# A fused two-block kernel: the attention part, the output projection, the last two norms and the second down product rewritten token-major

## The reference

```
h = rmsnorm(x, g_norm1) * (1 + sc1) + sh1
proj = h @ w_in                      # q 512, k 128, v 128, z 1024 columns
q, k = rope(rmsnorm(q, g_q)), rope(rmsnorm(k, g_k))      # per head of 64
attn = softmax(q k^T * 64 ** -0.5) v                     # 8 query heads, 2 key heads
u, v = split(gelu(z));  v = rmsnorm(v, g_tok_v)          # per head of 64
tok  = u * (w_s @ v + b_s)                               # in chunks of 128 tokens
mixed = concat(rmsnorm(attn, g_attn_out), rmsnorm(tok, g_tok_out))
x = x + gt1 * (mixed @ w_out)
h = rmsnorm(x, g_norm2) * (1 + sc2) + sh2
a, b = split(conv3(h @ w_up));  x = x + gt2 * ((silu(a) * b) @ w_down)   # 2816 wide
out = rmsnorm(x, g_final)
```

## Time and profile before

| | us |
|---|---|
| median of 3 runs | 857.83 |
| the profiled execution | 856.17 |
| its span, first to last instruction | 854.4 |
| PE busy in the span | 793.8 (93%) |
| DVE / ACT / POOL busy | 569.7 / 469.9 / 208.8 |
| mean granted clock of PE | 0.97 of full |

### The profile page before, as it was taken

The page is one execution under the profiler, slowest core; times in us unless marked ns, Lnnn a source line. Parts: engine busy times, 40 slices in busy tenths (PEclk is TensorE's granted clock), DMA queues, the critical chain, the costliest instruction groups (busy, mean ns, idle before and its releaser), DMA issues.

```text
span 854.4 us, 15196 instructions
## 1 busy us (share of the span) xinstructions
PE 793.8 (93%) x5717; PEld 735.8 (86%) x5717; DVE 569.7 (67%) x814; ACT 469.9 (55%) x757; POOL 208.8 (24%) x177
## 2 busy tenths in 40 slices
PE   3999999998999899999999988987797999999997
PEld 2899999987999689998989877865786999999997
DVE  7985777743776566675656656785536798866663
ACT  4975554466665465444454446656454555555553
POOL 4000000001024012253242314433253321233320
PEclk9999999999999979999999988999996999999998
DMA  6463332153445757787776812345151666555521
GB/s 240 135 186 126 124 123 101 50 174 99 129 163 178 270 198 272 245 271 265 276 274 242 315 54 99 99 173 173 49 172 50 221 230 213 185 187 185 185 98 50
DMA packets 45719, 146.97 MB, mean 172 GB/s; under 512 B 9292, under 2 KB 10060, under 8 KB 45664
## 3 DMA queue, kind: packets, MB, share of 16 engines
q1 hardware_dynamic: 44544, 144.88, 50.0%
q10 hardware_dynamic: 1120, 1.34, 0.5%
HBM read 144.07 MB, written 1.05 MB: 170 GB/s over the span
## 4 chain that ended last, share of the span: by engine, by line
PE 71%; issue 9%; DVE 9%; POOL 5%; ACT 4%; DMA 1%; POOLq 0%; SPq 0%; DVEq 0%; ACTq 0%
PE ps L736 23%; PE ps L492 19%; PE ps L749 7%; PE ps L690 7%; POOL gl L2151 2%; PE ps L961 2%; POOL relu L2148 2%; DVE ada_acc L1883 1%; PE ps L538 1%; PE ps L664 1%; PE ps L552 1%; PE ps L567 1%; DVE prob L1970 1%; PE ps L794 1%; DMA vtk<-in_x 1%
## 5 line engine op out<-in xcount | busy, mean ns | idle before, releaser
L1511 DVE TENSOR_TENSOR wl<-raw,wh 128x1024 fp32r<-128x1024 f32 x200 | 258.0, 1292 | 143.1 <-ACT wh L1023 141.8
L1023 ACT ACTIVATE wh<-raw 128x1024 fp32r<-128x1024 f32 x220 | 231.1, 1053 | 110.3 <-DMA raw<-in_w_stream 57.7
L736 PE MATMUL ps<-xh,wh 128*128 128x256 f32 x720 | 209.7, 291 | 12.6 <-POOL xl L2141 7.7
L736 PE MATMUL ps<-xl,wh 128*128 128x256 f32 x720 | 206.0, 286 | 0.0
L736 PE MATMUL ps<-xh,wl 128*128 128x256 f32 x720 | 206.0, 286 | 0.0
L736 PEld LDWEIGHTS ps<-xh,wh 128*128 128x128 f32 x720 | 139.8, 194 | 18.5 <-issue 11.6
L736 PEld LDWEIGHTS ps<-xl,wh 128*128 128x128 f32 x720 | 139.8, 194 | 1.3
L736 PEld LDWEIGHTS ps<-xh,wl 128*128 128x128 f32 x720 | 140.1, 195 | 0.0
L492 PE MATMUL ps<-xh,wh 128*128 128x256 f32 (+1 forms) x416 | 123.1, 296 | 2.2 <-DVE wl L1511 1.1
L492 PE MATMUL ps<-xh,wl 128*128 128x256 f32 (+1 forms) x416 | 119.0, 286 | 0.0
L492 PE MATMUL ps<-xl,wh 128*128 128x256 f32 (+1 forms) x416 | 118.9, 286 | 0.0
(11 more groups left out here) (389 smaller groups left out, 1472.9 us busy)
## 6 DMA issues: line engine op xcount, KB each, us to landing
raw<-in_w_stream SPq DMA_DIRECT2D x220, 512.0 KB, 3.7
ada_w<-in_w_ada SPq DMA_DIRECT2D x48, 512.0 KB, 4.5
vtk<-in_x SPq DMA_DIRECT2D x2, 512.0 KB, 4.8
out<-ob SPq DMA_DIRECT2D x4, 256.0 KB, 2.0
u<-uT SPq DMA_DIRECT2D x16, 34.0 KB, 2.4
eepp<-in_s_mats SPq DMA_DIRECT2D x1, 512.0 KB
bti<-btr SPq DMA_DIRECT2D x16, 32.0 KB, 2.5
ws<-in_w_s ACTq DMA_DIRECT2D x1, 512.0 KB, 3.8
```

The costliest lines, as they stand in the source:

```text
L736: mm = nc.tensor.matmul(ps[:, bank, 0:SEQ], w, x, start=(k == 0), stop=(k == 3 * KD - 1))
L1023: nc.scalar.activation(wh[:, b % RING], raw[:, b % RING], ACT.Identity).then_inc(hi_done, 1)
L1511: V.tensor_tensor(wl[:, b % RING], raw[:, b % RING], wh[:, b % RING].bitcast(F32), ALU.subtract).then_inc(lo_dve, 1)
```

## The change

Stages are named by their blocks: n counts from B_IN2, then from B_OUT2.

- Block order: gate values (n = 0 to 3) and gates (4 to 7) first, then v, k, q. The gelu is applied as each block leaves PSUM. The token mix runs behind n = 9.
- The remainders of the 20 blocks are made by DVE; POOL has nothing in this part.
- The query's deviation isn't multiplied into q. It is got by two matmuls of two columns per tile (`q_stat`), as 128x2 numbers per token, and enters as the scale of the exponential and of the maxima. The key norm stays.
- Heads go in pairs. `scores(i)` issues for both token halves the even head (partitions 0 to 63) and the odd head (64 to 127) in turn. The probabilities aren't divided; `weigh_v` gives tokens on the partitions (8 matmuls of 64 columns per pair), `attended` divides, and `turn_attended` turns the result back (2 transposes per pair). Pairs 0 to 3 stand in slots n = 12 and 13 of the first half and n = 0 to 4 of the output projection.
- The output projection is token-major (12 matmuls of 512 columns a block), first the gate branch (n = 0 to 3), then the attention branch (n = 4 to 7), each in two halves of the columns. The branch norm is a per-token scale, applied with the gate row gt1 as the product leaves PSUM (`out2`, `gated_part`, `add_part`). For it `turn_y` transposes the residual into `y_tm`, and `gate_row` spreads gt1 over the partitions.
- Norm r2 and the last norm are token-major, by squares with an accumulator on ACT (`row_squares`); r2 uses `turn_normed` and `split` as n1 does.
- The second down product uses `rows_in`, and gt2 is spread by two matmuls. g_final comes as a row by DMA.
- SP issues the modulation's weights in other slots of the loop (`ADA_SHARE[q - 2]`, `ada_rows`).

The diff, cut to its core:

```diff
+OUT2_BANKS = ((0, 1), (0, 1), (6, 7), (4, 5))
-POOL2 = (B_IN2 + AHEAD, B_F2)
@@ PE
+            def q_stat(i):
+                for t in range(NT):
+                    mm = nc.tensor.matmul(ps[:, 2, 256 + 2 * (NT * i + t):258 + 2 * (NT * i + t)], qs[:, (i + 1) % 3, t * P:(t + 1) * P],
+                                          heads2, start=True, stop=True)
+            def scores(i):
+                    pe.wait_ge(S["exp_done"], 2 * i)
+                for t in range(NT):
+                    for n in range(2):
+                        r = 64 * n
+                        mm = nc.tensor.matmul(ps[:, 6 + n, t * SEQ:(t + 1) * SEQ], qf[r:r + 64, i, t * P:(t + 1) * P], k,
+                                              start=True, stop=True)
             for b in range(B_IN2, B_OUT2):
+                if n in (1, 2):
+                    turn_y(n - 1)
+                if n == 4:
+                    turn_zv(0)
+                    turn_zv(1)
+                if n == 5:
+                    gate_row()
+                if n == 12:
+                    swap_k()
+                    tok_ms()
+                    q_stat(1)
+                    scores(0)
+                if n == 13:
+                    q_stat(2)
+                    scores(1)
+                    turn_probs(0)
+                    turn_probs(1)
             for b in range(B_OUT2, B_F2):
+                if n == 2:
+                    pe.wait_ge(S["part_done"], NT)
+                def one(t, kk):
+                    pe.wait_ge(S["branch_lo"], QT * branch + k + 1)
...
+                if n < 2:
+                    scores(n + 2)
+                if n < 3:
+                    turn_probs(2 * n + 2)
+                    turn_probs(2 * n + 3)
+                if n < 4:
+                    weigh_v(n)
+                if 1 <= n < 5:
+                    turn_attended(n - 1)
-                down(B_F2 + 3 * j + 1, j - 1, "ff2_lo", i * 4 + j, i * 12, first=(j == 1))
+                rows_down(B_F2 + 3 * j + 1, j - 1, "ff2_lo", i * 4 + j, F2_BANKS, i * 12, first=(j == 1))
@@ ACT
-                                         bias=smax[:, h, 1, t:t + 1], scale=HD ** -0.5,
+                                         bias=smax[:, h, 1, t:t + 1], scale=q_scale[:, h // 2, t, h % 2:h % 2 + 1],
+            def square_sum(src, to):
+                nc.scalar.activation(*src, ACT.Square, accum_out=to).then_inc(act_step, 1)
@@ DVE
+            def attended(i):
+                step(V.reciprocal(ssum[:, 2 * i:2 * i + 2, :], ssum[:, 2 * i:2 * i + 2, :]))
+                V.tensor_tensor(ao[:, i, :].rearrange("p (t h e) -> p t h e", t=NT, h=2),
...
+            def gated_part(t, bank, branch, dh):
+                V.scalar_tensor_tensor(pieces[t], ps[:, bank, :], branch_rstd[:, NT * branch + t:NT * branch + t + 1],
+                                       gate1[:, dh * 512:(dh + 1) * 512], ALU.mult, ALU.mult).then_inc(S["part_done"], 1)
+            def add_part(t, dh, counts):
+                dve.wait_ge(S["part_done"], parts[0])
+                ins = V.tensor_tensor(y_tm[:, t, dh * 512:(dh + 1) * 512], y_tm[:, t, dh * 512:(dh + 1) * 512], pieces[t], ALU.add)
             for b in range(B_OUT2, B_F2):
+                if n in (2, 3, 4, 5):
+                    att_lo(n - 2)
+                if n < 3:
+                    maxima(2 * n + 2)
+                    maxima(2 * n + 3)
+                if 1 <= n < 5:
+                    attended(n - 1)
+                if n == 2:
+                    out2(1, 0, 0)
+                if n == 4:
+                    out2(3, 0, 1)
+                lo(b + AHEAD)
+                if n == 6:
+                    out2(5, 1, 0)
@@ POOL
-            for b in range(POOL2[0], B_OUT2 + AHEAD):
-                lo(b)
```

More of the change, by code:

```diff
@@ L316, in two_blocks @@
[L316 to L323, removed]
+            "s_done", "max_done", "exp_done", "pt_done", "pt_copied", "o_done", "ao_done", "ao_turned",
@@ L714, in _ @@
                 rows_in(b, mh[:, k, :], ml[:, k, :], WO_BANKS, last=(b == B_F1 - 1))
-            turn_normed("n1")
-            def sum_squares(tag, bank, n=KD, per=1):
-                for m in range(n):
-                    pe.wait_ge(*norm(tag, "sq", m // per + 1))
-                    mm = nc.tensor.matmul(ps[:, bank, 0:SEQ], ones, sq[:, m, :], start=(m == 0), stop=(m == n - 1))
-                mm.then_inc(NORM["var"], 1)
+            turn_normed("n1", (ln("n1", "norm_act"), ln("n1", "norm_act", 2), ln("n1", "norm"), ln("n1", "norm_act", 3)))
             def block(b, bank, name, value, t=0, h=xh, l=xl, first=META, order=range(KD), ready=None):
@@ new lines, in _ @@
+                if n == 4:
[3 more added lines that the diff above has]
+                    gate_row()
+                if n == 8:
+                    pe.wait_ge(S["row_ev"], 2)
+                    modulation(1, (NMOD - 1) * KD, None, 0, 5)
+                if n == 9:
+                    turn_v2()
+                    for m in range(QT):
+                        mix_tokens(m)
+                if n == 10:
+                    k_stat()
+                if n == 11:
+                    q_stat(0)
@@ L969, in up2 @@
+            turn_normed("r2", (ln("r2", "norm_act"), ln("r2", "norm_act", 2), ln("r2", "norm"), ln("r2", "norm", 2)))
             def up2(j, i=0, ready=None):
@@ new lines, in _ @@
+            for t in range(NT):
+                row_squares(t, 0)
+            for t in range(NT):
+                row_squares(t, 1)
+                row_root(t)
+            for half in range(2):
+                act.wait_ge(*ln("r2", "rstd"))
+                nc.scalar.activation(xn[:, 0, half * 512:(half + 1) * 512], y_tm[:, 0, half * 512:(half + 1) * 512], ACT.Identity,
+                                     scale=row_rstd[:, 0:1]).then_inc(LN["norm_act"], 1)
+            split("r2", tg_m, lambda m: gain[:, 1, m:m + 1], lambda m: mod[:, M_SH2 + m:M_SH2 + m + 1])
@@ L2049, in outer_taps @@
+            row_reciprocal("r2", 0)
+            row_reciprocal("r2", 1)
+            dve.wait_ge(*ln("r2", "rstd", 2))
+            for half in range(2):
+                V.tensor_scalar(xn[:, 1, half * 512:(half + 1) * 512], y_tm[:, 1, half * 512:(half + 1) * 512], row_rstd[:, 1:2], None, ALU.mult)\
+                    .then_inc(LN["norm"], 1)
+            split("r2", tg_m, lambda m: gain[:, 1, m:m + 1], lambda m: mod[:, M_SH2 + m:M_SH2 + m + 1])
             def outer_taps(j, i, which):
```

811 lines of the change are left out of this document (407 added, 404 removed).

## The result

The changed kernel takes 835.77 us (median of 4 runs, 831.28 to 837.25) against 857.74 before (4 runs, 856.32 to 859.41): ratio 0.9734, 95% interval 0.9693 to 0.9776. Five more runs of it, beside eleven of the kernel before, gave 835.77 again, the kernel before 854.60: ratio 0.9781, 0.9754 to 0.9807. Forecast were 842.3 in a range of 836.5 to 851.0, so the time fell out of the range at its fast end, by 0.7 us.

The account below looks back on a forecast made before the run. PE mostly bounds the kernel; its waits in attention and projection, norm r2 and the end can move. -9.6-3.3-0.9-1.7 = -15.5 off the profiled 856.17 gives 840.7; the median is 1.7 above, so 842.3, range 836.5 to 851.

Parts of the forecast that it names:

- term 1: Attention and output projection: PE's own work -2.9 and its waits -6.7, together -9.6 us; bounds 0 to -15.
- Term 3: Down product of the second feed-forward: blocks of 2.80 for 2.84, 22 x 0.04 = -0.9 us; bounds 0 and -2.2.
- Term 4: The end, behind the last matmul: 11.3 us in place of 13.0, -1.7; bounds 0 and -3.
- small ones: Attention and projection: two PE waits, for the swapped key's copy and pair 2's exponentials, 0.7 us together.
- the long wait: Output block 2 waits 5.2 us for block 0's banks; 1.7 of clock lost behind it, as much as before.
- the right mirror: Token mix, outputs alternating between column halves, ran side by side; taken for the scores: 4.2 us in place of 8.4.
- Term 2: Norm r2 to the first down block: 13.1 us lost in place of 16.4, -3.3; bounds 0 and -6.1.
- rival 1: Attention scores: the pairs run one behind the other, 3.8 of the 4.2 us come back: 846.1; chance 0.27.
- rival 2: Attention: waits only move, the pair chain costs PE 15.5 us as before: 851.9; chance 0.13.
- rival 3: Output projection: the loop at output block 2 closes in each of slots 2 to 5, three more waits: 863.0; chance 0.05.

Follow-up runs that it names:

- the combination: The changed kernel with four edits of order (gated sums first, last remainder behind the last sum, exponential table loaded early): 825.77 us, ratio to before 0.9653.
- The run with GpSimd: The changed kernel with the remainders of the 19 weight blocks on GpSimd again, as before: 845.37 us, ratio to before 0.9875.

## Why the prediction was right and wrong

**The forecast's mechanism held; its sum was 2.4 too small. The step that failed is the size of PE's own work in term 1: -2.9 forecast, -4.5 measured.** Terms 3 and 4 were 0.6 and 0.8 short as well; the waits fell by 0.6 less than I had. One by one:

- Waits: 8.8 forecast, 9.0 measured, all at places that I had named. (Before they were 15.5 in the first trace and 14.1 in the second, so on average PE's idle time fell by 6.1, not 6.7.) By place they were less exact, so the good total is partly luck: block 2 4.6 for 5.2, block 5 1.6 for 2.0, the second pair 0.3 for 0.9, the copy of the swapped key none; but the fourth pair, which waits for the exponentials of pair 2, 2.4, where the two "small ones" together had 0.7. There I missed that the last query deviations make ACT load the root's table and then the exponentials' again, 1.28 each; the combination took 1.4 of it away.
- The clock behind the long wait: I had it cancel, and it did. The block behind the first wait of the output projection took 4.44 before (behind 2.8 us of waiting, clock 0.62) and 4.45 now (behind 4.6, clock 0.61).
- Score pairs: 4.2 saved forecast; four pairs of 1.07 (starts) against eight heads of 1.05: 4.1. The token mix was the right mirror, and the run with both heads on one half shows that the halves do it. The Trainium skill, TensorE: Matmul & The Clock Gate, Part 3, has it that matmuls on different row groups of the array run concurrently. The traces agree: 1.07 for a pair on two halves, in either order, 1.92 to 2.02 on one.
- Work, the step that failed: -2.9 forecast. PE's busy time fell by 4.5 (104.1 and 105.7 before, 99.7 and 101.0 after) though its clock was a little lower. `gate_row`: 2.1 by the scores' price; from its start to the next instruction's, 537.43 to 538.75, is 1.3. Products of 64 partitions and 256 columns gave no price for one of 128 partitions and 512 columns. The token mix went from 2.8 to 2.0 of busy time and the query statistics from 3.1 and 3.5 to 2.7; neither stood in my list at all. Against them an output block takes 2.88, not 2.80, in four of the eight (+0.3), and the sums that went (L939) had 3.9 of busy time, not 4.2.
- VectorE's load: I said that the division would lose its stall, gave that no price, and looked for harm only in the load. The run with GpSimd puts 10 us on it. It is inside the forecast because I built the waits from unstalled durations, so the sum had it without naming it. (The remainders that moved are 19, blocks 135 to 153, not 20.)
- Term 2: -3.3 forecast, -3.4 measured, partly by luck. The lag counted from VectorE's list was 1 too long (the second half's reciprocal started 5.0 behind PE's last end, at 627.44, not 6.15), and what stands behind it took 0.8 longer than in n1.
- Term 3: -0.9 forecast, -1.5 measured. The down blocks gave what I said. The up blocks followed in part: 20 rounds of 0.026 are 0.5, where the bound had 1.3. The spread of gt2 took 1.3, not 2.1, and the modulation that it replaces 1.7; but the stretch ends 0.3 later behind the start of the last down block (3.36 for 3.08).
- Term 4: -1.7 forecast, -2.5 measured. VectorE's sums ended 4.1 behind the last matmul for my 4.6, at 0.69 each for 0.75. The root of the second half ended 6.25 behind it for 6.95: the first root, with its table, ended at 4.2 for 4.5, and two squares and the second root took 2.0 for 2.45.

Rows of the end, VectorE and ACT:

```profile
826.65 0.69 DVE L2215 TENSOR_TENSOR res<-res,qg 128x512 f32<-128x512 f32 x1
...
829.50 0.16 DVE L2157 RECIPROCAL hb<-hb 128x1 f32<-128x1 f32 x1 [0.41 <-ACT hb L1413]
829.70 1.41 DVE L2221 SCALAR_TENSOR_TENSOR ob<-res,hb,wst 128x512 f32<-128x512 f32 x2
```

```profile
825.86 1.28 ACT L1413 ACT_TABLE_LOAD   x1
827.15 0.29 ACT L1413 ACTIVATE hb<-hb 128x1 f32<-128x1 f32 x1
```

**The rest of the miss is mostly the reference.** 842.3 less 835.8 is 6.5: 2.4 of it is the sum above, 0.8 the start. The remaining 3.3 are about what the kernel before varies by: 15.5 off 857.8 is 842.3, but the same kernel had medians of 854.6, 855.0 and 855.6 in three later sets of eleven runs. By the second ratio, 0.9781 x 857.8 = 839.0, which the range holds. So it is partly chance that the time fell below the range.

**The low end of the range was also added up wrongly.** It was to be term 1 without the clock loss (-1.7) and with half the waits (-4.4), and term 3 at its bound (-1.3). That is 842.3-7.4 = 834.9, not 836.5, and the measured 835.77 lies above it.

**The rivals.** Series pairs (rival 1): excluded, 1.07 a pair. Waits only move (rival 2): they fell from 15.5 to 9.0. The closing loop (rival 3): not here; block 2 alone waits for its banks, and block 5 only 1.6, for its low part. But a loop is what the kernel before shows when VectorE takes the remainders, by another chain. The longest wait came at output block 2, ended by the `qg` of L2043, with 4.6 for "near 5". One thing in it was wrong: I took the wait as given by the dependences. It was given by a list, and one line moved takes it away.

## What to carry over

When a wait is found, look at the engine that ends it for idle time ahead of the chain, and at what in its list could run there: here 8 us of idle stood in front of two instructions that were ready. A step that waits for another engine (a remainder for its high part) must not stand ahead of a chain that the other engine waits for. And whether a part of a change pays depends on the rest: the same 19 instructions cost 11 us in one order and save 10 in the other, so undo a part in the new kernel and add it alone to the old one.

## What the runs showed of the hardware

- VectorE beside a remainder of GpSimd (128 x 1024 from two operands in SBUF, most of them 2.34 to 2.41): an instruction on two numbers a partition that starts beside it ends when it ends, 1.63 to 2.23 in place of 0.16, three times of three. So in these three the cost was what was left of the remainder, not the size of the instruction. Row maxima read from PSUM (L2024) beside the same remainders kept their 0.68. In the other direction, a modulation row that began 0.04 behind a remainder took its usual 1.28, and the remainder 3.55.
- Float32 products of 64 partitions that lie on different halves run side by side: 1.07 for four of 256 columns, in either order of issue, and 1.9 to 2.0 when all are on one half.
- A wait of 4.6 us of PE was paid twice: the twelve matmuls behind it took 4.45 at a granted clock of 0.61 (0.50 for the first 3.5 us), and 2.9 where no wait stood ahead of them. Behind the wait of 6.7 they took 5.25, all at 0.50.
- The same program reached one point 4.1 us apart in two traces, half of it in the 16 sums of the norm (5.87 and 3.90). A forecast to within 1 us per stretch needs the stretch, not the total.
